# Differential attention in a hybrid layer: the 2176 keys of a score tile cut as 1024, 768 and 384 instead of 1024, 1024 and 128

## The reference, cut to what matters

```python
def one(qblk):
    s = jnp.einsum('bqhmd,bkhmd->bhmqk', qblk, k).astype(jnp.float32) * scale
    p = jax.nn.softmax(s, axis=-1)
    a = p[:, :, 0] - lam * p[:, :, 1]
    return jnp.einsum('bhqk,bkhe->bqhe', a.astype(v.dtype), v)
```

## Time and profile before

| | before |
|---|---|
| median of 3 runs | 1703.24 us |
| the profiled execution, its own time | 1703.68 us |
| its span in the profile | 1701.9 us |
| TensorE (PE) busy | 1641.9 us, 96% |
| VectorE (DVE) busy | 1039.8 us, 61% |
| ScalarE (ACT) busy | 854.7 us, 50% |
| GpSimd (POOL) busy | 766.4 us, 45% |
| attention, first to last product of scores | 833.5 to about 1471 us |

### The profile page before, as it was taken

How to read it: one execution, slowest core, us unless ns; L and a number is a source line. 1 busy time by engine, 2 the same in 40 slices (tenths; PEclk the granted TensorE clock), 3 DMA queues, 4 the chain that set the end, 5 groups by cost and what they waited for, 6 DMA issues and landing times.

```text
span 1701.9 us, 25279 instructions
## 1 busy us (share of the span) xinstructions
PE 1641.9 (96%) x8462; PEld 1447.5 (85%) x8462; DVE 1039.8 (61%) x1527; ACT 854.7 (50%) x1791; POOL 766.4 (45%) x807
## 2 busy tenths in 40 slices
PE   4999999999999999999879999999999999999999
PEld 1778999999999999999758788888888888888999
DVE  2553676663343343332479988878888888676662
ACT  3664666640010100000279988888888888722210
POOL 0001988960000000000078999999999899800000
PEclk8999999999999999999989999999999999999999
DMA  9663323342131132113332223114211111154541
GB/s 369 220 198 109 112 98 120 110 142 82 62 113 47 64 105 82 58 36 103 104 71 88 79 54 87 40 31 85 61 31 40 57 33 51 71 206 173 179 155 48
DMA packets 126907, 169.04 MB, mean 99 GB/s; under 512 B 10752, under 2 KB 113152, under 8 KB 125952
## 3 DMA queue, kind: packets, MB, share of 16 engines
q1 hardware_dynamic: 121712, 163.85, 29.9%
q10 hardware_dynamic: 5136, 4.46, 0.8%
HBM read 118.20 MB, written 50.07 MB: 99 GB/s over the span
## 4 chain that ended last, share of the span: by engine, by line
PE 82%; DVE 7%; DMA 4%; ACT 3%; SPq 1%; issue 1%; POOL 1%; DVEq 0%; ACTq 0%; POOLq 0%
PE ps L751 40%; PE ps L895 14%; PE ps L884 12%; PE ps L997 10%; PE ps L876 6%; DVE stt L1662 2%; DMA scr<-in_xT 1%; DMA xt<-in_xtok 1%; DMA scr<-in_xtok 1%; DVE e L1644 1%; DVE csr L1721 1%; DMA out_y<-yo 1%; DVE wo L1629 1%; ACT scr L1076 0%; ACT e L1255 0%
## 5 line engine op out<-in xcount | busy, mean ns | idle before, releaser
L751 PE MATMUL ps<-hT,w 128*128 128x448 f32 (+1 forms) x3360 | 676.4, 361 | 0.3 <-DVE w L1367 0.2
L751 PEld LDWEIGHTS ps<-hT,w 128*128 128x128 f32 x3360 | 621.3, 188 | 49.0 <-DVE w L1367 1.1
L1662 DVE TENSOR_REDUCE stt<-ps 128x1 f32<-128x1024 f32 x256 | 312.3, 1220 | 94.5 <-PE ps L895 92.2
L895 PE MATMUL ps<-kb,qb 128*128 (+1 forms) x1280 | 332.5, 390 | 15.4 <-ACT e L1255 8.2
L1255 ACT ACTIVATE e<-ps,stt 128x1024 f32<-128x1024 f32 x256 | 285.5, 1115 | 96.6 <-DVE stt L1662 96.2
L884 PE MATMUL ps<-at,vb 128*128 128x256 f32 x1088 | 276.5, 380 | 0.6 <-ACT atto L1212 0.5
L705 POOL TENSOR_TENSOR stt<-stt,lamc 128x2 f32<-128x2 f32 x64 | 12.5, 195 | 524.3 <-DVE stt L1687 524.3
L895 PEld LDWEIGHTS ps<-kb,qb 128*128 128x128 f32 x1280 | 204.9, 192 | 45.1 <-ACT e L1255 9.8
L884 PEld LDWEIGHTS ps<-at,vb 128*128 128x128 f32 x1088 | 201.0, 190 | 38.4 <-issue 1.3
L711 POOL TENSOR_TENSOR e<-e,stt 128x512 f32<-128x512 f32 (+1 forms) x192 | 209.2, 1090 | 5.0
L1163 ACT ACTIVATE scr<-ps 128x448 f32<-128x448 f32 (+1 forms) x40 | 20.8, 532 | 326.3 <-PE ps L751 326.3
(11 more groups left out here) (140 smaller groups left out, 1656.5 us busy)
## 6 DMA issues: line engine op xcount, KB each, us to landing
raw<-in_w_in SPq DMA_DIRECT2D x32, 512.0 KB, 4.0
qb<-spill_q SPq DMA_DIRECT2D x256, 64.0 KB, 2.3
wad<-in_w_ada SPq DMA_DIRECT2D x4, 2048.0 KB, 17.1
scr<-in_xT SPq DMA_DIRECT2D x8, 1024.0 KB, 6.2
raw<-in_w_gate SPq DMA_DIRECT2D x16, 512.0 KB, 4.0
spill_k<-scr SPq DMA_DIRECT2D x32, 224.0 KB, 2.1
spill_q<-scr SPq DMA_DIRECT2D x32, 224.0 KB, 2.2
mixc<-spill_cv SPq DMA_DIRECT2D x8, 896.0 KB, 9.5
```

The costliest lines, as they stand in the source:

```text
L751: mm = pe.matmul(out, slot_of(l, j), rhs_of(r, j), start=(i == 0 and j == 0), stop=(i == 2 and j == DJ - 1))
L895: mm = pe.matmul(out[:, c0 - k0:c1 - k0], qb[:, t, ver, m], keys, start=(ver == 0), stop=(ver == 1))
L1662: dve.tensor_reduce(stt[:, b, 0, 3 * m + c:3 * m + c + 1], ps[:, 2 * c:2 * c + 2, :].rearrange("p c n -> p (c n)"), AX.X, ALU.max, negate= ...
```

## The change

The sample's 2176 keys are cut at 1024 and 1792 instead of at 1024 and 2048. Piece 0 stays as it is (1024 keys in banks 0 and 1, two products 512 wide). Piece 1 has 768 keys, as two products 384 wide that lie against the border between the banks 2 and 3. Piece 2 has 384 keys and one product 384 wide, in bank 4. Since bank 4 then has no room for both maps, they take turns: TensorE makes map 0's at the end of part 1, and map 1's at the end of part 2, after a wait on the exponential of map 0's. The maxima and the exponentials follow: map 0's at the start of part 2 and map 1's at the start of part 3, each ahead of the part's own. GpSimd's six scalings and two additions are cut evenly (384 and 576 wide). The seventeenth transpose moves to the last 128 columns of bank 4. The loads of the first head's keys are counted on two semaphores in another way.

```diff
-PIECES = [(0, 1024), (1024, SAMPLE), (SAMPLE, KEYS)]
-PARTS = [(1, 1024, 1536), (1, 1536, SAMPLE), (2, SAMPLE, KEYS)]
+PIECES = [(0, 1024), (1024, 1792), (1792, KEYS)]
+WIDE = [512, 384, 384]
+PARTS = [(1, 1024, 1408), (1, 1408, 1792), (2, 1792, KEYS)]
...
+        def pair(c):
+
+            k0, k1 = PIECES[c]
+            both = ps[:, 2 * c:2 * c + 2, :].rearrange("p c n -> p (c n)")
+            return both[:, N - WIDE[c]:N - WIDE[c] + k1 - k0]
...
-                for i, (k0, k1) in enumerate(((1024, 1536), (1536, KEYS))):
-                    pool.wait_ge(e1_done, 3 * n + 1 + 2 * i)
-                    pool.wait_ge(e0_done, 3 * n + 1 + 2 * i)
+                for i, (k0, k1) in enumerate(((1024, 1600), (1600, KEYS))):
+                    pool.wait_ge(e1_done, 3 * n + 2 + i)
+                    pool.wait_ge(e0_done, 3 * n + 2 + i)
...
-                    for c0 in range(k0, k1, N):
-                        c1 = min(c0 + N, k1)
+                    for c0 in range(k0, k1, WIDE[c]):
+                        c1 = c0 + WIDE[c]
...
                             if isinstance(n, int) and n == 0:
-                                pe.wait_ge(s_k0, 32 * (NG - 2))
+                                pe.wait_ge(s_k0, 32 * (NG - 1))
                             elif t == 0:
-                                pe.wait_ge(s_k, 96 + 64 * (it // 4))
-                        if isinstance(n, int) and n == 0 and p == 1:
-                            pe.wait_ge(s_k, 96)
+                                pe.wait_ge(s_k, 64 + 64 * (it // 4))
                         wait(pe, exp_done, 4 * n + p - 1)
-                        pair = ps[:, 2 * (p % 2):2 * (p % 2) + 2, :].rearrange("p c n -> p (c n)")
-                        scores(it, t, pair, p // 2, *PIECES[p % 2]).then_inc(s_pair, 1)
+                        scores(it, t, pair(p % 2), p // 2, p % 2).then_inc(s_pair, 1)
...
                     if sc and p == 1:
-                        wait(pe, expc_done, n)
+                        if isinstance(n, int) and n == 0:
+                            pe.wait_ge(s_k, 64)
+                        wait(pe, expc_done, 2 * n)
                         wait(pe, t_act, 4 * (n - S_TR))
-                        scores(it, t, ps[:, 4, 0:P], 0, SAMPLE, KEYS)
-                        scores(it, t, ps[:, 4, P:2 * P], 1, SAMPLE, KEYS).then_inc(s_ctx, 1)
+                        scores(it, t, ps[:, 4, 0:WIDE[2]], 0, 2).then_inc(s_ctx, 1)
+                    if sc and p == 2:
+                        pe.wait_ge(expc_done, 2 * n + 1)
+                        scores(it, t, ps[:, 4, 0:WIDE[2]], 1, 2).then_inc(s_ctx, 1)
...
-                    if sc and p == 3:
-                        act.wait_ge(mxc_done, n + 1)
-                        wait(act, a1_ready, n - 1)
-                        for mc in range(2):
-                            dst = e0[:, t] if mc == 0 else e1[:, b]
-                            em = act.activation(dst[:, SAMPLE:KEYS], ps[:, 4, mc * P:(mc + 1) * P], ACT.Exp,
-                                                bias=stt[:, b, 0, 3 * mc + 2:3 * mc + 3],
-                                                accum_out=stt[:, b, 1, 3 * mc + 2:3 * mc + 3])
-                        em.then_inc(expc_done, 1)
+                    if sc and p >= 2:
+                        mc = p - 2
+                        act.wait_ge(mxc_done, 2 * n + 1 + mc)
+                        if mc:
+                            wait(act, a1_ready, n - 1)
+                        dst = e0[:, t] if mc == 0 else e1[:, b]
+                        act.activation(dst[:, PIECES[2][0]:KEYS], ps[:, 4, 0:WIDE[2]], ACT.Exp,
+                                       bias=stt[:, b, 0, 3 * mc + 2:3 * mc + 3],
+                                       accum_out=stt[:, b, 1, 3 * mc + 2:3 * mc + 3]).then_inc(expc_done, 1)
...
+                    if sc and p >= 2:
+                        dve.wait_ge(s_ctx, 2 * n + p - 1)
+                        dve.tensor_reduce(stt[:, b, 0, 3 * p - 4:3 * p - 3], ps[:, 4, 0:WIDE[2]], AX.X, ALU.max,
+                                          negate=True).then_inc(mxc_done, 1)
...
-                    if sc and p == 2:
-                        dve.wait_ge(s_ctx, n + 1)
-                        dve.tensor_reduce(stt[:, b, 0, 2:6:3], ps[:, 4, 0:2 * P].rearrange("p (m k) -> p m k", m=2), AX.X,
-                                          ALU.max, negate=True).then_inc(mxc_done, 1)
```

More of the change, by code:

```diff
@@ L371, in trbank @@
             cnt = TGROUPS[g][1]
-            return ps[:, 5 + g % 2, 0:cnt * P] if g < 4 else ps[:, 4, 2 * P:(2 + cnt) * P]
+            return ps[:, 5 + g % 2, 0:cnt * P] if g < 4 else ps[:, 4, 3 * P:(3 + cnt) * P]
+        def pair(c):
+            k0, k1 = PIECES[c]
+            both = ps[:, 2 * c:2 * c + 2, :].rearrange("p c n -> p (c n)")
+            return both[:, N - WIDE[c]:N - WIDE[c] + k1 - k0]
         @block.sync
@@ L555, in _ @@
                         sp.wait_ge(z_mm, CV0 + CV_UNITS * f + CV * (tg + 1))
-                        first_keys(c0, c0 + n, c0, s_k0 if tg < TG - 1 else s_k)
+                        first_keys(c0, c0 + n, c0, s_k0)
                         if tg > 0:
@@ L887, in product, with scores @@
                     mm.then_inc(pv_mm, 1)
-            def scores(it, t, out, m, k0, k1):
+            def scores(it, t, out, m, c):
+                k0, k1 = PIECES[c]
                 for ver in range(2):
-                    for c0 in range(k0, k1, N):
-                        c1 = min(c0 + N, k1)
+                    for c0 in range(k0, k1, WIDE[c]):
+                        c1 = c0 + WIDE[c]
                         keys = kb[:, 0, m, c0:c1] if isinstance(it, int) else \
@@ L904, in step @@
                             if isinstance(n, int) and n == 0:
-                                pe.wait_ge(s_k0, 32 * (NG - 2))
+                                pe.wait_ge(s_k0, 32 * (NG - 1))
                             elif t == 0:
-                                pe.wait_ge(s_k, 96 + 64 * (it // 4))
-                        if isinstance(n, int) and n == 0 and p == 1:
-                            pe.wait_ge(s_k, 96)
+                                pe.wait_ge(s_k, 64 + 64 * (it // 4))
                         wait(pe, exp_done, 4 * n + p - 1)
-                        pair = ps[:, 2 * (p % 2):2 * (p % 2) + 2, :].rearrange("p c n -> p (c n)")
-                        scores(it, t, pair, p // 2, *PIECES[p % 2]).then_inc(s_pair, 1)
+                        scores(it, t, pair(p % 2), p // 2, p % 2).then_inc(s_pair, 1)
                     if p == 0 and tr_last:
                         if sc or n == NT:
-                            pe.wait_ge(expc_done, n)
+                            pe.wait_ge(expc_done, 2 * n)
                         transposes(n - 1 - S_TR, (t - 1 - S_TR) % 4, 4)
@@ L1254, in step @@
                         dst = e0[:, t] if m == 0 else e1[:, b]
-                        act.activation(dst[:, c * 1024:(c + 1) * 1024],
-                                       ps[:, 2 * c:2 * c + 2, :].rearrange("p c n -> p (c n)"), ACT.Exp,
+                        act.activation(dst[:, PIECES[c][0]:PIECES[c][1]], pair(c), ACT.Exp,
                                        bias=stt[:, b, 0, 3 * m + c:3 * m + c + 1],
@@ L1661, in step @@
                             wait(dve, coef_done, n - 1)
[L1662 to L1663 removed]
+                        dve.tensor_reduce(stt[:, b, 0, 3 * m + c:3 * m + c + 1], pair(c), AX.X, ALU.max,
                                           negate=True).then_inc(mx_done, 1)
@@ L1688, in step @@
                     if p == 3 and sc:
-                        dve.wait_ge(mxc_done, n + 1)
+                        dve.wait_ge(mxc_done, 2 * n + 2)
                         dve.wait_ge(mx_done, 4 * n + 4)
```

2 lines of the change are left out of this document (removed).

## The result

The changed kernel takes 1728.08 us, the median of four runs (1726.26 to 1730.11); four runs of the kernel before beside them have 1703.59 (1698.88 to 1707.0). The ratio is 1.015, with an interval of 1.0136 to 1.0165. The profiled execution took 1726.26 us with a span of 1724.5, 22.6 longer than the span before.

What follows compares the result with a forecast made beforehand. In the steady attention only what TensorE is fed was taken to cost time. A wait of 0.69 less 0.21 saved gives 0.48 a step; 60 steps make 28.8 us, so 1703.7 + 29 gives 1733 us, range 1717 to 1750.

Steps and rivals of the forecast that it cites:

- The wait, its place and its size: TensorE before map 1's third piece, end of part 2: waits for map 0's third exponential, 0.69 us in every steady step.
- The bounds of 0.37 and 1.12: ScalarE's exponential of 384 columns: estimated 0.59 us, between the rows for 128 and 1024 columns; waits of 0.48 and 1.22.
- What the widths save: TensorE's scores: 3.94 us a step for 4.15, so 0.21 less, 13.4 us for 64 steps.
- A step: Steady attention step: 0.69 of wait less 0.21 saved makes it 0.48 us longer, 9.95 for 9.47.
- The early steps: First four steps charged nothing, the other 60 charged 0.48 us each; the eight with w_out blocks allowed 4 us either side.
- At nothing: Other effects, no cost: map 1's third piece has 1 us of cover; VectorE's extra reduction is hidden; GpSimd's columns are unchanged.
- the third rival: Same wait feeds back as a second, at part 0's transpose or part 1's scores: 0.53 more a step, 1765 us; chance 7%.
- The clock in steady steps: Sign in a window of steady steps: the granted clock stays 1.00.
- the rival of a lower clock: Idle times of 0.7 us bring spells of half clock on TensorE: 48 us, about 1780; chance 2%.
- the table of waits: Sign: TensorE waits for L1252 about 40 us in all, about 0.7 us in each of about 60 steps.
- the weight load: TensorE's products 128 wide: a load of 128 columns, 107 ns by the skill's page, would explain their 113.

Runs made afterwards that it cites:

- exponential-first kernel: Changed kernel with map 0's third exponential on ScalarE right behind part 1's, ahead of the scaling and the copy: 1710.47 us, ratio 1.0035.
- best kernel: Changed kernel with map 1's third piece behind part 3's scores and map 0's third exponential ahead of the copy, behind the scaling: 1693.35 us, ratio 0.9942.
- kernels without splitting: Kernel before and changed kernel, each with w_out's splitting and loading moved behind the loop: steps 4 to 15 took 118.96 and 121.64 us.
- product-later kernel: Changed kernel with map 1's third piece on TensorE behind part 3's scores, not ahead of them: 1698.52 us, ratio 0.9966.
- kernel with the turns only: Kernel before with its widths (1024, 1024, 128), but the maps' third pieces take turns in bank 4: 1759.46 us, ratio 1.0324.

## Why the prediction was right

**The wait, its place and its size: right.** The forecast was 0.69 a step in L903 behind L1252, of which 0.08 for the start and the slower first run. Measured are 0.64 to 0.65 from start to start, and the run of six behind it takes 1.14 to 1.18 instead of 1.12 (the exponential-first kernel, without the wait): 0.66 to 0.69 together. The chain held term by term, set against the step above: part 1's maximum 0.96 (forecast 0.95), the exponential 0.90 (0.91), scaling and copy unchanged, and the copy to the third exponential 0.48. Of the exponential of 384 columns, the one term without a row of its own, the groups say (1005 to 1450 us: count, busy, mean ns):

```profile
L1264 ACT ACTIVATE e<-ps,stt 128x768 f32<-128x768 f32 x88 | 79.4, 902 | 9.5 <-DVE stt L1674 6.4
...
L1252 ACT ACTIVATE e<-ps,stt 128x384 f32<-128x384 f32 x86 | 50.8, 591 | 0.0
...
L1690 DVE TENSOR_TENSOR stt<-stt 128x6 f32<-128x6 f32 x44 | 6.8, 155 | 0.0
```

591 ns, where the straight line through 128 and 1024 columns gave 0.59. The bounds of 0.37 and 1.12 had been wide out of care; the value between them was right.

**What the widths save: right.** Part 1's scores went from 1.02 to 0.785, 0.235 less (forecast 0.23); map 0's third piece with part 2's scores from 1.453 to 1.353, 0.10 less (0.10); map 1's piece adds 0.124 to part 3's (0.35 less the 0.23). The best kernel shows the sum, 0.21 a step, in the time. The Trainium skill, "TensorE: Matmul & The Clock Gate", section "Back-to-back issue gap", has a formula, N / 2.4 + 2.5 ns for a product N wide, by which these sums would be 0; the trace disagrees, as it did before the change. The prediction read it as the price in a stream of products. The section gives it for a product by itself, says that it counts too little at small N because it has no weight load, and puts a stream at about 81 ns for 128 columns and 131 for 512; the rows have 113 and 231, so the trace agrees with neither.

**A step: right.** 9.47 and 9.90 became 9.95 and 10.35, in steps 16 to 62 on average 0.485 more (forecast 0.48). Where the loop turns it is 10.52 instead. The third exponential ends 7.59 after the step's start there and not 7.50, and TensorE starts 0.14 behind its end and not 0.05; why it does is open. These steps were longer before the change too, 9.99 on average against 9.90. So their growth is 0.53, 0.07 more than that of the other steps with nine products or 0.8 us in all, which the forecast did not have. The wait, once there, takes on small delays of the chain.

**The early steps: the mis-sized term.** The forecast charged 60 steps with 0.48, 28.8 us, and gave the steps with splitting 4 us to either side. Measured, the 47 steps from 16 on cost 22.8 us (47 x 0.48 is 22.6), and steps 4 to 15 only 0.6 where 5.8 stood; with steps 0 to 3 at -0.8 and the rest at +0.1 that is the 22.6 between the spans, and the time came out 5 us under the forecast. There are two causes. First, in steps 5 to 15 TensorE already waited before the change for what the splitting delayed. Part 1's transposes and the scores behind them, before and after, in step 8 (start, length):

```profile
926.97 0.60 PE L876 MATMUL ps<-cst,e 128*128 128x128 f32 x4
927.77 1.64 PE L895 MATMUL ps<-kb,qb 128*128 x8 [0.20 <-ACT at L1204]
```
```profile
924.99 0.60 PE L883 MATMUL ps<-cst,e 128*128 128x128 f32 x4
925.54 1.54 PE L903 MATMUL ps<-kb,qb 128*128 x6
...
929.11 1.30 PE L903 MATMUL ps<-kb,qb 128*128 x6 [0.73 <-ACT e L1252]
```

0.80 before the change, 0.44 over the usual distance, of which 0.19 is left after it: TensorE now waits behind these scores and has less to wait for at them. Summed over steps 5 to 15, this place lies 2.9 us over the usual distance before the change and 0.6 after it. It is not all gain: in the changed kernel the wait at map 1's third piece sums to 9.1 us in these steps, and to 6.9 without the splitting. The kernels without splitting show the balance: the splitting costs steps 5 to 15 of the kernel before 5.8 us and of the changed one 3.1, so the change costs 2.3 there and not the 5.0 that it costs without. Second, step 4 took 12.12 before and 10.34 after, for the clock. The windows with its first 4 us, of before and of after (clock third from the end):

```profile
881.00:885.00 4.00, 3.98 (x10) 3.02 (x11) 1.86 (x3) 0.60 (x1) 0.07 (x1) 0.50 0.24 68
```
```profile
880.20:884.20 4.00, 4.00 (x21) 3.48 (x22) 2.71 (x6) 1.52 (x4) 1.04 (x3) 1.00 0.30 87
```

At 0.50, the level of 1.2 GHz, ten products fit in where 21 do at 1.00. Whether the change shifted this spell or chance did is open: such spells lie elsewhere in each trace. It is why the share of the first cause is told from steps 5 to 15 alone. The 1.8 us of step 4 may be chance. Without them the spans would lie 24.4 us apart, nearer to the forecast, so chance did not help it.

**At nothing: right.** Map 1's third exponential ended 1.3 us ahead of the transpose that needs its bank, where the forecast had 1 us (1208.41 in the step above, and the transpose comes 1.01 behind the scores of 1208.70). The feedback of the third rival did not come in this kernel, and it did in the exponential-first kernel, at the very place that the rival named: part 0's transpose. GpSimd's row, for the earlier trace rows, has more slack than before:

```profile
1202.34 0.20 POOL L712 TENSOR_TENSOR stt<-stt,lamc 128x2 f32<-128x2 f32 x1 [1.33 <-DVE stt L1698]
```

**The clock in steady steps: right.** 0.64 us of idle in every step of 10 us left it at 1.00, and the rival of a lower clock fell.

**In the table of waits** about 40 us had been forecast; 34.3 stand there, for the modelled ends told of above.

## What to carry to other kernels

Where two users take turns in a buffer, the price is not how long the buffer is in use but what stands in the queue ahead of the instruction that frees it; work out both arrival times in one step's timeline before the change is made. If the wait is there, move the one who asks later and the one who frees earlier, each by only as much as nothing else waits for: here moving past a copy was free, and past a scaling it came back through VectorE. And a new wait costs less in steps where the engine waits already (2.3 us and not 5.0 here), so the steps with other work on the queues are to be read apart.

## What the runs showed of the hardware

**VectorE and GpSimd hold each other up, one whole instruction at a time.** VectorE's product of 128 x 6 numbers took 155 ns on average (1005 to 1450 us) in the changed kernel, 194 before, 270 in the product-later kernel and 527 in the best one, the shape being the same each time. In the rows of the product-later kernel the long one, of 0.43, ends as GpSimd's sums end. `combine`, of 1024 columns, waits in the same way for the GpSimd instruction that is under way when it comes. The changed kernel, for the 1.92 of the exponential-first one:

```profile
1205.26 0.83 POOL L721 TENSOR_TENSOR e<-e,stt 128x384 f32<-128x384 f32 x1
```
```profile
1205.80 1.36 DVE L1652 SCALAR_TENSOR_TENSOR e<-e,stt 128x1024 f32<-128x1024 f32 x1
```

Counted from the end of GpSimd's instruction, `combine` took 1.07 here (1206.09 to 1207.16) and 1.08 there (1064.46 to 1065.54). What differs is how much of that instruction was left when it came, 0.29 and 0.84. GpSimd's next one, L721 there, took 1.81 and not 0.83 while `combine` ran. The Trainium skill, "SBUF — State Buffer", section "SBUF: two separate sides", says that a VectorE instruction with two inputs from SBUF and a GpSimd one share a port pair under an exclusive lock for a whole instruction; the rows agree, 0.43 for 0.16 and 1.81 for 0.83. GpSimd has less slack in the best kernel (296.65 of 320.00 us busy, 278.12 in the changed one), and the small product is longest there. But it is not only a matter of the step's length: `combine` has means of 1391, 1495, 1684 and 1759 in the changed kernel, the product-later one, the one before and the best one, and 1899 in the kernel with the turns only, whose steps are the longest. Whether this is the next limit no run here tests.

The window of the best kernel, 1160 to 1480 us, beside that of the changed one:

```profile
1160.00:1480.00 320.00, 319.21 (x1795) 280.01 (x1794) 277.21 (x393) 283.50 (x646) 296.65 (x333) 1.00 0.20 56
```

**A narrow float32r product costs more than its columns.** 128 columns cost 0.113 us, 384 cost 0.174 and 512 cost 0.231, so from 512 to 384 the time falls with the columns, and at 128 it is twice the third of 0.174. In the attention part 1's four products fell by 0.235 from 512 to 384 columns, four times the difference of 0.057. What holds the price up at 128 columns no run here shows; the weight load, which the prediction names for it, stays an explanation.
